# Moving a gated norm into the end of a delta-rule stage, and loading the next weights during that stage

## What is computed

```python
o, s = _gated_delta_rule(q, k, v, g, beta, s0)
o = _rmsnorm(o, o_gain) * jax.nn.silu(z.reshape(B, T, GDN_HEADS, GDN_DV))
y = o.reshape(B, T, GDN_V_W) @ w_out
return y, xp[:, -(CONV_W - 1):], s      # xp: the rows ahead of the convolution
```

## Time and profile before

| what | us |
|---|---|
| median of 3 runs | 1725.44 (1724.85 to 1726.69) |
| the profiled execution, its own time | 1723.49 |
| its span, first to last instruction | 1721.8 |
| PE busy | 1597.5 (93%) |
| DVE busy | 1163.5 (68%) |
| ACT busy | 962.6 (56%) |

### The profile page before, as it was taken

How to read it: one execution, slowest core, us unless ns; L and a number is a source line. 1 busy time by engine, 2 the same in 40 slices (tenths; PEclk the granted TensorE clock), 3 DMA queues, 4 the chain that set the end, 5 groups by cost and what they waited for, 6 DMA issues and landing times. The chain is left out here.

```text
span 1721.8 us, 25618 instructions
## 1 busy us (share of the span) xinstructions
PE 1597.5 (93%) x10468; PEld 1339.5 (78%) x10468; DVE 1163.5 (68%) x1234; ACT 962.6 (56%) x1176; POOL 103.9 (6%) x193
## 2 busy tenths in 40 slices
PE   5999889867999997997779999999999999999997
PEld 3999465757999997995576788888888888888884
DVE  3775621268444456345774888888888888888887
ACT  2553422266333435333565777777777777777775
POOL 2210100000000000000002001010101000000021
PEclk8999999978999998999987999999999999999999
DMA  9720989373554354339035999999999999999995
GB/s 326 226 74 19 366 319 382 128 221 99 153 153 147 124 158 148 99 99 366 39 104 178 343 360 378 369 374 379 364 382 359 386 363 377 369 376 363 367 381 187
DMA packets 267610, 447.92 MB, mean 260 GB/s; under 512 B 12662, under 2 KB 125519, under 8 KB 267471
## 3 DMA queue, kind: packets, MB, share of 16 engines
q1 hardware_dynamic: 263132, 431.59, 72.1%
q0 software_dynamic: 3632, 13.11, 2.0%
q10 hardware_dynamic: 720, 1.50, 0.3%
HBM read 421.68 MB, written 24.48 MB: 259 GB/s over the span
## 5 line engine op out<-in xcount | busy, mean ns | idle before, releaser
L2778 DVE TENSOR_TENSOR w_lo_late<-raw,w_hi_late 128x2048 fp32r<-128x2048 f32 x262 | 597.8, 2290 | 102.6 <-ACT w_hi_late L2630 100.9
L2630 ACT ACTIVATE w_hi_late<-raw 128x2048 fp32r<-128x2048 f32 x262 | 502.0, 1916 | 156.5 <-PE bank L356 155.4
L354 PE MATMUL bank<-w_hi_late,hg_hi 128*128 128x512 f32 (+1 forms) x768 | 292.1, 380 | 0.8 <-DVE w_lo_late L2778 0.8
L356 PE MATMUL bank<-w_hi_late,hg_lo 128*128 128x512 f32 (+1 forms) x768 | 289.8, 377 | 0.0
L355 PE MATMUL bank<-w_lo_late,hg_hi 128*128 128x512 f32 (+1 forms) x768 | 288.1, 375 | 0.0
L275 DVE TENSOR_TENSOR w_lo_main<-raw,w_hi_main 128x2048 fp32r<-128x2048 f32 (+1 forms) x50 | 112.4, 2250 | 89.0 <-ACT w_hi_main L268 89.0
L356 PEld LDWEIGHTS bank<-w_hi_late,hg_lo 128*128 128x128 f32 x768 | 144.5, 188 | 29.1
L355 PEld LDWEIGHTS bank<-w_lo_late,hg_hi 128*128 128x128 f32 x768 | 144.5, 188 | 28.9
L354 PEld LDWEIGHTS bank<-w_hi_late,hg_hi 128*128 128x128 f32 x768 | 144.3, 188 | 28.9 <-DVE w_lo_late L2778 1.2
L354 PE MATMUL bank<-w_hi_late,act_hi 128*128 128x512 f32 x352 | 141.3, 402 | 0.5 <-DVE w_lo_late L2778 0.5
L356 PE MATMUL bank<-w_hi_late,act_lo 128*128 128x512 f32 x352 | 139.8, 397 | 0.0
(11 more groups left out here) (528 smaller groups left out, 2812.6 us busy)
## 6 DMA issues: line engine op xcount, KB each, us to landing
raw<-in_moe_w_gate SPq DMA_DIRECT2D x88, 1024.0 KB, 7.1
raw<-in_moe_w_up SPq DMA_DIRECT2D x88, 1024.0 KB, 7.1
raw<-in_moe_w_down SPq DMA_DIRECT2D x88, 1024.0 KB, 6.3
ada_delta<-in_ada_w SPq DMA_DIRECT2D x40, 1024.0 KB, 8.5
raw<-in_gdn_w_in SPq DMA_DIRECT2D x16, 1024.0 KB, 10.6
slot_rows_far<-zero_row SPq DMA_DIRECT2D x1, 12288.0 KB, 38.8
raw<-in_ffn_w_gate SPq DMA_DIRECT2D x22, 512.0 KB, 4.0
raw<-in_ffn_w_up SPq DMA_DIRECT2D x22, 512.0 KB, 5.3
```

The source lines that it names most:

```text
L354: pe.matmul(out, w_hi, x_hi, start=start, stop=False)
L356: return pe.matmul(out, w_lo, x_hi, start=False, stop=stop)
L2630: act.activation(k.w_hi[:, m % SPL, :], k.raw[:, m % RAW, :], ACT.Copy).then_inc(k.hi_ready, 1)
L2778: dve.tensor_tensor(k.w_lo[:, m % SPL, :], k.raw[:, m % RAW, :], k.w_hi[:, m % SPL, :], ALU.subtract).then_inc(k.raw_split, 1)
```

## The change

The block of the gated norm is gone; its work is put into the lists of the delta stage, in five pieces by token blocks and heads: piece 0 is unit S (all heads, 64 tokens), pieces 1 and 2 are unit 0 (four heads each), pieces 3 and 4 are unit 1. The outputs of unit S are computed right after the state step of unit 0, ahead of the state-key product of unit 1; the outputs of unit 1 go to other banks and are signalled by halves. ACT squares each piece straight from the bank; DVE multiplies bank, gain and `silu(z)` in one instruction ahead of the root, and by the root later; the copies to `yT` and the root's own DVE pass with the gain go. The last modulation turn is moved ahead, and ACT then waits until PE has read all of the modulation ring, because `w_hi` and `w_lo` now exist during the stage. ACT splits the first two `w_out` slabs there, DVE the first. SP loads three `w_out` slabs as soon as the scratch under them is free, and the fourth a little later. The final states lie at another place in `raw`. PE turns the convolution rows at the end of the stage, four groups side by side on the partitions of one bank; DVE copies them in the output projection (six copies of 6 x 512), and SP stores them in twelve pieces there, after the loads of slabs 4 to 9.

```diff
 # mixed_phase, SyncE
+            if row_out is not None:
+                sp.wait_ge(k.stores[0], k.n_store[0])
+                k.load(sp, n0 + 4)
+                k.load(sp, n0 + 5)
             for n in range(n0, n0 + n_slabs):
                 k.load(sp, n + RAW)
-            if stored:
+            if row_out is not None:
+                sp.wait_ge(sig["copied"].sem, copied0 + QKV_T // 4)
+                for q in range(QKV_T // 4):
+                    for s in range(2):
+                        rows = slice(32 * (q % 4) + 3 * s, 32 * (q % 4) + 3 * s + 3)
+                        k.store(sp, 0, k.o["conv"][s][0, 0][:, 512 * q:512 * q + 512], row_out[rows, q // 4, :])
                 sp.wait_ge(k.stores[0], k.n_store[0])
 # mixed_phase, VectorE
                 k.ahead_lo(dve, n0 + s + AHEAD)
+                if s == 0 and row_out is not None:
+                    for q in range(QKV_T // 4):
+                        rows = slice(32 * (q % 4), 32 * (q % 4) + 6)
+                        dve.tensor_copy(row_out[rows, q // 4, :], k.ps[6 + q // 4][rows, :]).then_inc(sig["copied"].sem, 1)
                 if s == 0:
                     for kt in range(1, KT):
...
 # delta_phase, SyncE
+            sp.wait_ge(join_done, 2)
+            for n in range(3):
+                k.load(sp, n_out + n)
+            sp.wait_ge(join_done, 4)
+            sp.wait_ge(xy_ready, len(steps))
+            k.load(sp, n_out + 3)
 # delta_phase, TensorE
             per_head((b[5], b[6]), k_tail[0], v_tok[0]).then_inc(s_done, 1)
             k.ada_pe(pe, 1)
+            pe.wait_ge(u_ready, 1)
+            for h in range(H):
+                pe.matmul(by64(b[2])[:, h, :], state[1][:, h, :], q_of(S)[:, h, :], start=True, stop=False)
+                last = pe.matmul(by64(b[2])[:, h, :], v_tok[S][:, h % 4, :], at_of(S)[:, h, :], start=False, stop=True)
+            last.then_inc(o_done, 1)
             pe.wait_ge(join_ready, 4)
             pe.wait_ge(s_ready, 1)
             per_head((b[1], b[7]), k_of(1), state[0]).then_inc(ks_done, 1)
+            k.ada_pe(pe, 99)
...
+            def norm_sum(n):
+                pe.wait_ge(squared, squared0 + n + 1)
+                pe.wait_ge(gated, gated0 + min(n, 2) + 1)
+                if n >= 3:
+                    pe.wait_ge(logs, logs0 + n - 1)
+                pe.matmul(sum_bank[n][:], k.ones[:], sq[n], start=True, stop=True).then_inc(summed, 1)
+
+            norm_sum(0)
+            pe.wait_ge(u_ready, 3)
             pe.wait_ge(s_ready, 2)
             per_head((b[5], b[6]), k_tail[1], v_tok[1]).then_inc(s_done, 1)
...
+            norm_sum(1)
+            norm_sum(2)
+            for half in range(2):
+                for h in range(4 * half, 4 * half + 4):
+                    bank = by128((b[1], b[7])[half])
+                    pe.matmul(bank[:, h % 4, :], state[0][:, h, :], q_of(1)[:, h, :], start=True, stop=False)
+                    last = pe.matmul(bank[:, h % 4, :], v_tok[1][:, h, :], at_of(1)[:, h, :], start=False, stop=True)
+                last.then_inc(o_done, 1)
+            norm_sum(3)
+            norm_sum(4)
+            pe.wait_ge(s_ready, 3)
+            pe.wait_ge(gated, gated0 + 5)
+            for q in range(QKV_T // 4):
+                part = slice(32 * (q % 4), 32 * (q % 4) + 6)
+                for j in range(4):
+                    pe.matmul(b[6 + q // 4][part, j * P:(j + 1) * P], last_rows[:, 4 * q + j, :], k.ident[:], start=True, stop=True)
 # delta_phase, VectorE
             last.then_inc(s_ready, 1)
+            k.ada_dve(dve, 99)
...
+            gate(0)
             dve.wait_ge(ks_done, 2)
             residue(1, (b[1], b[7]))
             dve.wait_ge(s_done, 2)
             add_state(1, S, state[1], last_state[1])
+            k.ahead_lo(dve, n_out)
+            gate(1)
+            gate(2)
+            normed(0)
             dve.wait_ge(s_done, 3)
             add_state(0, 1, state[0], last_state[0])
-            k.ada_dve(dve, 99)
+            low(0)
+            gate(3)
+            normed(1)
+            normed(2)
+            gate(4)
+            low(1)
+            low(2)
+            normed(3)
+            normed(4)
+            low(3)
+            low(4)
 # delta_phase, ScalarE
+            k.ada_act(act, 99)
...
+            act.wait_ge(k.ada_read, 7 * ADA_GROUP)
+            k.ahead_hi(act, n_out)
+            square(0)
+            k.ahead_hi(act, n_out + 1)
+            square(1)
+            square(2)
             act.wait_ge(u_done, 3)
             rows_out(1, (b[1], b[7]))
+            invert(0)
+            high(0)
+            square(3)
+            invert(1)
+            invert(2)
+            square(4)
+            high(1)
+            high(2)
+            for n in (3, 4):
+                invert(n)
+            for n in (3, 4):
+                high(n)
```

More of the change, by code:

```diff
@@ L717, in dve, with mixed_phase @@
             dve.tensor_tensor(self.lo[:, kt, :], self.src[:, kt, :], self.hi[:, kt, :], ALU.subtract).then_inc(self.k.sig["lo"].sem, 1)
-def mixed_phase(k, n0, n_slabs, n_k, x_hi, x_lo, gate, gain, sums, renewal, stored=False):
+def mixed_phase(k, n0, n_slabs, n_k, x_hi, x_lo, gate, gain, sums, renewal, row_out=None):
     nc, sig = k.nc, k.sig
@@ L731, in mixed_phase @@
     part0 = take["part"](3)
+    copied0 = take["copied"](QKV_T // 4) if row_out is not None else 0
     y_sum, r_y = k.squares[:, 2, :], k.squares[:, 2, :]
@@ L1152, in delta_phase @@
         state_in, cleared = sem("state_in"), sem("inv_cleared")
+        sig = k.sig
+        squared, squared0 = sig["squared"].sem, sig["squared"].take(5)
+        gated, gated0 = sig["added"].sem, sig["added"].take(5)
+        summed, summed0 = sig["summed"].sem, sig["summed"].take(5)
+        logs, logs0 = sig["logs"].sem, sig["logs"].take(5)
+        root, root0 = sig["root"].sem, sig["root"].take(5)
+        scaled, scaled0 = sig["scaled"].sem, sig["scaled"].take(5)
+        hi_done, hi_done0 = sig["hi"].sem, sig["hi"].take(5)
+        lo_done, lo_done0 = sig["lo"].sem, sig["lo"].take(5)
+        n_out = k.first["w_out"]
         block = mem.enter_context(nc.Block())
@@ L1532, in _, with gate, normed, low @@
             last.then_inc(s_ready, 1)
+            k.ada_dve(dve, 99)
+            def gate(n):
+                dve.wait_ge(squared, squared0 + n + 1)
+                dve.scalar_tensor_tensor(piece(oT, n), shaped(from_bank[n][:], n), k.vec_b[:, 72:73], piece(z_silu, n), ALU.mult,
+                                         ALU.mult).then_inc(gated, 1)
+            def normed(n):
+                dve.wait_ge(root, root0 + n + 1)
+                dve.wait_ge(gated, gated0 + n + 1)
+                dve.tensor_tensor(piece(oT, n), piece(oT, n), shaped(inverse[n], n), ALU.mult).then_inc(scaled, 1)
+            def low(n):
+                dve.wait_ge(hi_done, hi_done0 + n + 1)
+                dve.tensor_tensor(piece(lo, n), piece(oT, n), piece(hi, n), ALU.subtract).then_inc(lo_done, 1)
+            gate(0)
             dve.wait_ge(ks_done, 2)
@@ L1640, in _, with square, invert @@
             rows_out(0, (b[3], b[4]))
[L1641 to L1644, removed]
+            k.ada_act(act, 99)
+            def square(n):
+                act.wait_ge(o_done, (1, 2, 2, 3, 4)[n])
+                act.activation(sq[n], from_bank[n][:], ACT.Square).then_inc(squared, 1)
+            def invert(n):
+                act.wait_ge(summed, summed0 + n + 1)
+                act.activation(inverse[n], sum_bank[n][:], ACT.Ln, scale=1.0 / DK, bias=k.eps[:]).then_inc(logs, 1)
+                act.wait_ge(logs, logs0 + n + 1)
+                act.activation(inverse[n], inverse[n], ACT.Exp, scale=-0.5).then_inc(root, 1)
@@ L1645, in _, with high @@
+            def high(n):
+                act.wait_ge(scaled, scaled0 + n + 1)
+                act.activation(piece(hi, n), piece(oT, n), ACT.Copy).then_inc(hi_done, 1)
+            act.wait_ge(k.ada_read, 7 * ADA_GROUP)
[4 more added lines that the diff above has]
+            square(2)
             act.wait_ge(u_done, 3)
             rows_out(1, (b[1], b[7]))
-            act.wait_ge(o_done, 2)
-            for half in range(2):
-                act.activation(oT[:, 4 * half:4 * half + 4, P:TP], by128(b[3 + half]), ACT.Copy)
@@ L2975, in sb @@
                 return gdn.enter_context(nc.sbuf_tensor(name, shape, dt))
-            z_silu = sb("z_silu", [P, H, T])
+            with nc.sbuf_tensor("z_silu", [P, H, T], F32) as z_silu:
+                pass
+            o_lo = sb("o_lo", [P, H, T], F32R)
             last_rows = sb("last_rows", [P, QKV_T, 6])
-            with nc.sbuf_tensor("qkv", [P, QKV_T, T], F32) as qkv, \
-                    nc.sbuf_tensor("lnb", [P, GC], F32) as lnb, nc.sbuf_tensor("g", [P, GC], F32) as g:
+            with nc.sbuf_tensor("qkv", [P, QKV_T, T], F32) as qkv:
+                pass
+            sb("q_place", [P, H, T])
+            o_hi = sb("o_hi", [P, H, T], F32R)
+            sb("v_place", [P, H, T])
```

(1 more changed line is left out.)

118 lines of the change are left out of this document (19 added, 99 removed).

## The result

| | before | changed |
|---|---|---|
| median us | 1725.14 (1722.07 to 1726.69, 4 runs) | 1709.82 (1708.99 to 1712.61, 4 runs) |
| profiled execution, its own time | 1723.49 | 1708.99 |
| its span | 1721.8 | 1707.3 |

The ratio of the times is 0.9919, with a 95% interval of 0.9902 to 0.9935: faster by 15 us. Forecast were 1710.9 us and a range of 1705.5 to 1717.5.

What follows compares the result with a forecast made beforehand. PE was taken to bound the kernel, with DVE's list limiting the projection's gain. Profiled 1723.49 less 14.5 gives 1709.0; with 1.95 from execution to median, the forecast was 1710.9 us, range 1705.5 to 1717.5.

Steps and rivals of the forecast that it cites:

- Start of the projection's block: End of the delta stage: following the new lists, the output projection's block starts at 351.1 us, before at 364.99.
- my lower bound: Projection's block start if every hand-over between engines overlaps by 0.1 us: 349.7 us.
- The interleaving: Delta stage: norm work and two moved steps among PE's products push its own last products back by 6.9 us.
- Inside the projection: Output projection: 21.2 us to slab 3's low split, copies eating what splits freed, then 17.0 to the add at 389.3.
- PE's gain that turns into a wait: Output projection: PE starts 17.9 us earlier, but about 3 us become a wait for DVE's sums; the add gains 14.5.
- rival B: Output projection: DVE catches up, so PE's whole earlier start of 17.9 us comes through, giving 1707.5 us; chance 0.08.
- C: Norm's pieces run one after another behind unit 1's outputs; block starts 9.2 us later, gain 5.3, 1720.1 us; chance 0.14.
- D: The twelve stores hold the end of the projection's block until 394.0, 4.6 us lost, 1715.5 us; chance 0.07.
- E: Delta stage: the first weight slab lands late; each us beyond 3.8 of room is lost; chance 0.05, 0.03 of it slower.
- The clock: Half clock in the new tail puts the block's start at 353.8; at the projection's start, 3 us of waiting covers it.
- The table load: A load ahead of invert(0) would cost 1.3 us, delaying DVE 0.1; by the skill page 2.7 on ACT, 1.5 on DVE.
- A: Likeliest case: delta-stage overlap and DVE's projection list give 14.5 us, 1710.9 us, from 1707.5 to 1714; chance 0.66.

Runs made afterwards that it cites:

- the repetition: The changed kernel measured once more, unaltered, on another chip: 1708.34 us, ratio 0.9922 to the kernel before.
- the second pair: Changed kernel with five ACT instructions more, with slabs 0 and 1 split in the projection against not: 1715.83 against 1706.92 us.
- the kernel with the splits late: Changed kernel with w_out slabs 0 and 1 split in the output projection instead of the delta stage: 1722.96 us, ratio 0.9986.
- the two first disturbed kernels: Changed kernel with slabs 0 and 1 split in the projection, 1722.96 us; changed kernel with all norm work behind unit 1's outputs, 1724.27 us.
- all three kernels with the stall: Changed kernel with slab splits in the projection, 1722.96 us; with norm behind unit 1's outputs, 1724.27; with the sample unit's exponential written as two, 1719.23.
- five more: Changed kernel with five ACT instructions more, the delta stage's 128x512 exponentials each written as two of 128x256: 1706.92 us, ratio 0.9929.
- all three edits: Changed kernel with row copies on ACT, slab 2's high split ahead of the squares, and no table load at the projection's head: 1703.74 us, ratio 0.989.
- the copies on ACT: Changed kernel with the six convolution-row copies moved from DVE to ACT, behind the split of slab 2: 1703.62 us, ratio 0.9876.
- the two disturbed kernels with five more: Slab splits in the projection, and norm behind unit 1's outputs, each on the changed kernel with five ACT instructions more: 1715.83 and 1714.14 us.

## Why the prediction was right, point by point

**Start of the projection's block.** Forecast 351.1, measured 350.63, and this hides an error. From the last modulation unit to the block I counted 30.8 us (320.34 to 351.1) and it took 29.1 in every kernel whose edits leave the norm and the slabs in place: hand-overs overlap, even a little more than in my lower bound (349.7, or 29.4). What I took as an edge was the rule. It stayed unseen because the unit itself started at 321.53, 1.2 us later than in the profile before, behind the matmuls at a low clock shown above. It starts at 320.13 in the repetition and anywhere up to 323.93 in the others.

**The interleaving.** Outputs 1 were forecast for 339.2, 6.8 later than before; they start at 339.13. `residue` was forecast to end at 331.7 and ends at 331.90, and the low split behind `add_state` starts at 333.88 (333.9). Counted from the unit, though, `residue` ends 1.0 us and outputs 1 start 1.3 us sooner than forecast, so most of the 1.7 us lies in these first steps, and the interleaving put outputs 1 back by 5.6 us, not 6.8. ACT's closing chain, square(3) to high(4), ran from 341.12 to 349.58 (forecast 341.1 to 350.1), and ACT was the full engine there, as forecast.

**Inside the projection.** From the block's start to the low split of slab 3: 21.35 (forecast 21.2). The copies took 4.26 (4.1), and that they eat what the splits freed is shown by both edits: without the copies 4.3 us come back, and with the splits in the projection 3.8 are lost (4.9 in the second pair). From there to the add: 16.7 (17.0). The add stands at 388.64, forecast 389.3.

**PE's gain that turns into a wait.** PE starts 18.8 us earlier and the add 15.1. PE's gain turns into waits of 3.3 us for DVE's `squares` and 2.7 for ACT's `mix_sums`, where the waits of before show 0.9 at most. That is 6.0 and not the 3 us forecast: before, PE began the projection at a granted clock of 0.50 and had it for some 6 us (369.4 to 375.4), now it has 1.00 from the first matmul. By an estimate from these rows it saves half of that, 3 us, and waits for them as well. So rival B falls.

**The other rivals.** C asked for over 10 us of waits for sums and roots between 325 and 360 us. In the changed kernel DVE's waits for roots add up to 1.8 us, ACT has none of any length for a norm sum, and its longest wait at a norm pass is its 2.38 us for unit 1's outputs. Built on purpose, the serial form costs 6.5 us at the block and 7.3 at the add, not the 9.2 that I took from the old block's length, because ACT's passes of different pieces still overlap DVE's. D: the twelve stores took 4.19 us to issue (0.35 each, within the forecast 3 to 13), had issued by 379.5, and DVE's add was later by 9. E: ACT split slab 0 at 323.16 without waiting for a DMA.

**The clock.** I allowed for a low clock in the tail or at the projection's start. The granted clock stayed at 1.00 from 321 to 365 us, through PE's 1.58 us pause, and the first projection matmul took 0.39 us. The 5.97 us pause of the kernel with the splits late did bring the low clock: 0.50 behind it, and a first projection matmul of 0.63 us. The Trainium skill (TensorE: Matmul & The Clock Gate, Why this matters for your kernels) warns of idle gaps between bursts of matmuls; the long pause agrees with it, and the short one shows that not every pause has this effect, which the section does not claim. The pauses that do cost here are PE's waits of 3.3 and 3.4 us ahead of its closing sums, which I had only in the range, at 1 us.

**The table load.** The next ACT pass starts at 351.88, 1.29 us after the load's start. The drain that the Trainium skill (ScalarE: Activation LUTs, What ACT_TABLE_LOAD costs) adds is given for a switch to a different set, and neither this load nor the one at 342.71 that I compared with it is one: the set that they ask for is in place since about 169 us. A true switch, to the table for silu at 408.03, is followed by its pass at 409.38, 1.35 us later, so the drain does not show there either. No load stands ahead of invert(0), so that bound was never drawn.

**The range of A.** Its bounds do not follow from its own terms: 1710.9 less 1.4 and 1 is 1708.5, and with 2.7 and 1 it is 1714.6, where 1707.5 and 1714 are written. The measured 1709.8 lies in either.

The sum was right because each half was carried to the engine that ends last, not to the one whose wait vanishes. Its exactness is luck: in the stretch the change gave 16.3 us where 14.5 were forecast, and 1.7 of the 1.8 between them are the overlaps. Against them 1.2 us were lost ahead of the last modulation unit and 0.6 behind the add, both at a low clock, and so the errors cancel.

## What to carry to other kernels

When a wait of PE vanishes, price the gain at the list of the engine that is nearly as long: here 18.8 us at PE's start became 15.1, and six small copies on DVE held the end back by 4.3 more, which moving them to ACT gave back. Hand-overs between engines inside one block overlap; count the chain without a gap at each. And when a small edit costs far more than its stretch shows, look at the chain near the end for "issue" time: the instruction list may have moved, not the work.

## What the runs showed that I had not expected

One ACT instruction more, in the delta stage, made ACT stand still for 13 us at jumps 1.5 ms later. The pages do not name it in the two first disturbed kernels (their count for ACT, 1170, leaves semaphore instructions out), but the traces do: in all three kernels with the stall ACT's list has 1685 records. With 1684 (the changed kernel and two variants), 1689 (five more, and all three edits) and 1690 (the copies on ACT, and the two disturbed kernels with five more) there is none. So the stall goes with one length of ACT's list, and not with the edit's own work. Why this length is bad, and whether late fetching is the reason, as the packets of the instruction queue suggest, stays open. A median without a look at the last block would have blamed the splits for 13 us, of which 4 to 5 are theirs.
